# Reordering the SBUF tensors of a two-block transformer kernel (a 256-aligned layout against one whose large buffer starts 96 bytes off)

## The chip, the core and the metric

The kernel runs on one core of one Trainium2 chip, everything in float32 (indices in int32). The metric is the device time of one execution in microseconds, the median of several executions. Three executions of the kernel before took 2364.87, 2370.28 and 2371.98 us; the median is 2370.28 us.

## The reference, cut to what matters

Two blocks of two layers each run one after the other on 256 tokens of width 1024. The first block has a modulation (adaLN) from one conditioning vector, a mixer (pooling and windowed attention) and an expert layer in which each token fetches 128 experts by index; the second has four attention mixers and a dense MLP.

```python
for l in range(2):                                    # first block
    mod = silu(c) @ w_ada[l] + b_ada[l]               # 1024 x 6144
    h = rms_norm(x) * (1 + sc1) + sh1
    x = x + g1 * (mixer(h @ w_in[l]) @ w_out[l])
    h2 = rms_norm(x) * (1 + sc2) + sh2
    e, gate = peer_topk(h2 @ wq[l], subkeys[l])       # 128 experts for each token
    a = einsum('cd,ced->ce', h2, u[l][e])             # u, v: 16384 x 1024 each
    x = x + g2 * einsum('ce,ced->cd', gelu(a) * gate, v[l][e])
for l in range(2):                                    # second block
    x = x + mixers(rms_norm(x) @ w_in2[l]) @ w_out2[l]
    x = x + square(relu(rms_norm(x) @ w_up[l])) @ w_down[l]
return rms_norm(x)
```

## The kernel before, in words

The 256 tokens stand as two tiles of 128 partitions. Every SBUF tensor is declared once, at the start of `build` (L177 to L198), through `sb(name, n)`, which takes 128 partitions by `n` four-byte elements. The order of these declarations is the order in which the tensors lie in each partition. No tensor is reused through a pool that picks addresses; all views (`QK`, `RNG`, `HALF`, `S`, `kT`, `MT` and so on) are fixed slices of the declared tensors.

The largest tensor, `BIG`, holds 5120 elements of working space (`QK`) and then 12 slots of 2048 elements (`RNG`), 8 KB in each partition. A 13th slot is the first 2048 elements of `MOD`. Slots 0 to 7 and 13 take what GpSimd's queue fetches: first 48 blocks of `w_ada` (L447), then the expert rows (L454). One indirect DMA brings, for the 128 tokens of a tile, the row `uv[expert]`, which is the 1024 elements of `u` and the 1024 of `v`, 8 KB for each partition. There are 512 such fetches (4 passes of 128). Slots 8 to 11 take what SyncE loads (L325): the weights of the mixer and of the query projection, and in the second block all weights.

One expert step is: the row lands in a slot; VectorE forms the dot product of its first half with the token's `H` (L1620, output into `BIG`); ScalarE applies Gelu, the gate, and writes a diagonal matrix into `DG` (L1149, L966), reading the identity matrix that lies at the start of `CST`; TensorE multiplies the row's second half by that diagonal into PSUM (L513, two matmuls of 512 columns); then the slot is free and GpSimd issues the fetch that goes into it. The mixer and head steps of the next pass are interleaved with the expert steps by an order written out by hand (`WHEN`, `LATE`, `drive`). After the fourth pass the second block runs without gathers; its weights come through SyncE's queue into 12 slots in turn, two for each of the 16 MLP steps of a layer.

In the kernel before, `EPSC` takes 128 bytes at 16,512, and so `X` starts at 16,640, which is a multiple of 256. Every size up to and with `BIG` is a multiple of 256, so all of these start at one too. `PARB` does too, but its size isn't a multiple of 256, so `CST` (223,520) starts 32 bytes behind a multiple of 256 and `SC` (227,776) 192 behind one.

Of the kernel before, what the change touches and what calls it, by code (L numbers as in the profile page):

```python
# [20 lines left out]
PAR = 3720  # L21
# [3 lines left out]
C_ID, C_ND, C_ROPE, C_IOTA, C_SEL, C_END = 0, 128, 640, 1024, 1040, 1064  # L25
# [141 lines left out]
def build(nc, I, out):  # L167
    with ExitStack() as ctx:
        def sb(name, n, dt=F32):
            return ctx.enter_context(nc.sbuf_tensor(name, [128, n], dt))  # L170
# [1 line left out]
        T = Tally(lambda name: ctx.enter_context(nc.semaphore(name.replace(".", "_"))))  # L172
        up, at, last, landed = T.up, T.at, T.last, T.landed

        EPSC = sb("EPSC", 32)[:, 0:1]  # L177
        X = sb("X", 2048)[:, :].rearrange("p (t d) -> p t d", t=2)
        MOD = sb("MOD", 5120)[:, :]
        G2 = sb("G2", 1024)[:, :]  # L180
        ROWS = sb("ROWS", 256)[:, :]
        HT = sb("HT", 2048)[:, :].rearrange("p (c s) -> p c s", c=8)
        H = sb("H", 2048)[:, :].rearrange("p (t d) -> p t d", t=2)
        PRJ = sb("PRJ", 2560)[:, :]
        ONES = sb("ONES", 128)[:, :]
        ACC = sb("ACC", 1024)[:, :].rearrange("p (b n) -> p b n", b=2)
        DG = sb("DG", 4 * 128)[:, :].rearrange("p (b n) -> p b n", b=4)
        GATE = sb("GATE", 256)[:, :]
        AV = sb("AV", 256)[:, :]
        EID = sb("EID", 256, I32)[:, :]  # L190
        TV = sb("TV", 2 * 64)[:, :]
        TI = sb("TI", 2 * 64, U32)[:, :]
        TC = sb("TC", 256)[:, :]
        SKB = sb("SKB", 256)[:, :]
        BIG = sb("BIG", 5120 + SLOTS * SLOT)[:, :]
        PARB = sb("PARB", PAR)[:, :]
        CST = sb("CST", C_END)[:, :]
        SC = sb("SC", 384)[:, :]  # L198
        ZC = PARB[:, 384:888].rearrange("p (k m) -> p k m", k=8)
        CREP = PARB[:, 128:384].rearrange("p (k m) -> p k m", k=8)  # L200
        MC, BC, NC = PARB[:, 0:32], PARB[:, 32:64], PARB[:, 64:80]
        QK, RNG = BIG[:, 0:5120], BIG[:, 5120:5120 + SLOTS * SLOT]
        PS = ctx.enter_context(nc.psum_tensor("PS", [128, 8, 512], F32))

# [22 lines left out]
        S = QK[:, 4608:5120].rearrange("p (b i s) -> p b i s", b=2, i=2)  # L227
        prj1 = PRJ.rearrange("p (t n) -> p t n", t=2)
        g1, sh2, sc2 = (MOD[:, i * 1024:(i + 1) * 1024] for i in range(2, 5))
# [5 lines left out]
        AT = QK[:, 4096:5120].rearrange("p (b i s) -> p b i s", b=2, i=2)  # L235
        QF = PRJ[:, 0:768].rearrange("p (t i d) -> p t i d", t=2, i=4)
        KF = PRJ[:, 768:1536].rearrange("p (t i d) -> p t i d", t=2, i=4)
        VB = PRJ[:, 1536:2048].rearrange("p (t n) -> p t n", t=2)
        JD2 = PRJ[:, 2048:2304]
        RT, TMP = MOD[:, 0:1024], MOD[:, 1024:1344]  # L240
# [6 lines left out]
        def par1(k):  # L247
            return PARB[:, P1[k][0]:P1[k][0] + P1[k][1]]

# [68 lines left out]
        def sp_program(e):  # L318
# [33 lines left out]
            def head(l, t, h):  # L352
                if (l, t, h) == (1, 0, 0):
                    sp.wait_ge(*at("pe.sk", 0, 1, 7))
                    sp.e.dma_start(SKB, I["skT"][1]).then_inc(*landed("ld_sk", 1))
                if t == 0 or h > 1:
# [10 lines left out]
            sp.e.dma_start(G2[0:1, :], I["bada"][0:1, 5120:6144]).then_inc(*landed("ld_g2", 0))  # L367
            sp.e.dma_start(SKB, I["skT"][0]).then_inc(*landed("ld_sk", 0))
            sp.e.dma_start(ROWS[8:24, :], I["bada"][1:2, 2048:6144].rearrange("a (b n) -> (a b) n", n=256)).then_inc(*landed("ld_rows"))

# [138 lines left out]
        def pe_program(e):  # L509
# [34 lines left out]
            def spread(l, b, banks):  # L544
# [3 lines left out]
                if b < 8:  # L548
                    for c in range(2):
                        p = mm(PS[:, bk, 256 + c:257 + c], R[:, c * 128:(c + 1) * 128], ONES[:, 0:1], True, True)  # L550
                else:
                    p = mm(PS[:, bk, 256:512], ONES, R, True, True)
                p.then_inc(*up("pe.adb", l, b))
# [14 lines left out]
            def late():  # L568
# [3 lines left out]
                for c in range(2):  # L572
                    p = mm(PS[:, 2, 256 + c * 8:264 + c * 8], ROWS[:, c * 128:(c + 1) * 128], CST[:, C_SEL:C_SEL + 8], True, True)
                p.then_inc(*up("pe.adc"))
# [29 lines left out]
            def by_tokens(bk, t, w, width):  # L604
                wv = w[:, 0:8 * width].rearrange("p (k n) -> p k n", k=8)
                for k in range(8):
                    p = mm(PS[:, bk, 0:width], HT[:, k, t * 128:(t + 1) * 128], wv[:, k, :], k == 0, k == 7)
                return p
# [117 lines left out]
            def head(l, t, h):  # L726
                k = Clock()
                have_hT(l, t, 2)
                sk = SKB.rearrange("p (a n) -> p a n", a=2)
                wv = have(in_w, ("wq", l, t, h) if t == 0 or h > 1 else ("wq", l, 0, 7 - h)).rearrange("p (k n) -> p k n", k=8)  # L730
# [3 lines left out]
                for i in range(2):  # L734
                    yield from k.to(2 * i)
                    for c in range(8):
                        p = mm(PS[:, 7, i * 128:(i + 1) * 128], wv[:, c, i * 128:(i + 1) * 128],
                               HT[:, c, t * 128:(t + 1) * 128], c == 0, c == 7)
                p.then_inc(*up("pe.q", l, t, h))
# [7 lines left out]
            def experts(p, b):  # L747
# [9 lines left out]
                for hf in range(2):  # L757
                    m = mm(PS[:, hf, :], DG[:, (p * 128 + j) % 4, :], x[:, 1024 + hf * 512:1536 + hf * 512], j == 0, j == 127)
                m.then_inc(*up("pe.vsum", p, j))

            def project_A(l, t):
# [4 lines left out]
                for name, o, n in (("A0", 0, 192), ("A1", 192, 160)):  # L766
                    w = have(in_2, ("w2", l, name))[:, 0:8 * n].rearrange("p (k n) -> p k n", k=8)
                    for k in range(8):
                        p = mm(PS[:, bk, o:o + n], HT[:, k, t * 128:(t + 1) * 128], w[:, k, :], k == 0, k == 7)
                p.then_inc(*up("pe.A", l, t))  # L770
# [11 lines left out]
            def project(l, name, parts=(0, 1)):  # L782
# [11 lines left out]
                for z in parts:  # L794
                    zs = slice(z * 128, (z + 1) * 128)
                    for k in range(8):
                        if name in ("D0", "D1"):
                            p = mm(PS[:, bk, z * 256:(z + 1) * 256], w[:, k, zs], HT[:, k, :], k == 0, k == 7)
                        else:
                            p = mm(PS[:, bk, z * 256:(z + 1) * 256], HT[:, k, zs], w[:, k, :], k == 0, k == 7)  # L800
                if 1 in parts:
# [41 lines left out]
            def out2(l, s, t):  # L843
# [4 lines left out]
                for c in range(2):  # L848
                    for hf in range(2):
                        p = mm(PS[:, t * 2 + hf, :], HT[:, CHUNK[s] * 2 + c, t * 128:(t + 1) * 128], w[:, c, hf * 512:(hf + 1) * 512],  # L850
                               s == SECTIONS[0] and c == 0, s == SECTIONS[3] and c == 1)
# [110 lines left out]
        def act_program(e):  # L962
# [36 lines left out]
            def rms_in_hT(name, key, t, srcs, D):  # L999
# [5 lines left out]
                a.wait_ge(*last("a.c"))  # L1005
                a.e.activation(s, s, ACT.Sqrt, bias=EPSC, scale=1.0 / D).then_inc(*up("a.rms", *key))

            def rms(name, key, srcs, D, junk):
                s = sc(name, len(srcs))
                w = srcs[0].shape[-1]  # L1010
                for i, src in enumerate(srcs):
                    o = i * w % 1024
                    a.e.activation(junk[:, o:o + w], src, ACT.Square, accum_out=s[:, i:i + 1]).then_inc(*up("a.c"))
                    if o + w == 1024 or i == len(srcs) - 1:
                        a.wait_ge(*last("a.c"))
                a.e.activation(s, s, ACT.Sqrt, bias=EPSC, scale=1.0 / D).then_inc(*up("a.rms", *key))

# [38 lines left out]
            def pre(l, t):  # L1056
# [32 lines left out]
                a.wait_ge(*at("v.qks", l, t))  # L1089
                a.e.activation(s, s, ACT.Sqrt, bias=EPSC, scale=1.0 / 64).then_inc(*up("a.rms", "qk", l, t))  # L1090
                yield from k.to(WHEN["proj"] + 15)
# [31 lines left out]
            def head(l, t, h):  # L1123
# [9 lines left out]
                if n > 1:  # L1133
# [5 lines left out]
                a.wait_ge(*at("v.best", l, t, h))  # L1139
                a.e.activation(GATE[:, j:j + 16], V[:, 32:48], ACT.Exp, bias=V[:, 48:49], scale=1.0,  # L1140
                               accum_out=V[:, 49:50]).then_inc(*up("a.gate", l, t, h))

            def experts(p, b):
# [7 lines left out]
                a.wait_ge(*at("a.gelu", p, b - 1))  # L1151
                copy(AV[:, j:j + 1], AV[:, j:j + 1], GATE[:, j:j + 1]).then_inc(*up("a.gated", p, b - 1))
                if n > 3:
                    a.wait_ge(*at("pe.vsum", (n - 4) // 128, (n - 4) % 128))
                a.wait_ge(*at("a.gated", p, b - 1))
                copy(DG[:, n % 4, :], ident, AV[:, j:j + 1]).then_inc(*up("a.diag", p, b - 1))

# [11 lines left out]
            def latent(l, t):  # L1169
# [7 lines left out]
                a.wait_ge(*last("a.c"))  # L1177
                a.e.activation(s, s, ACT.Sqrt, bias=EPSC, scale=1.0).then_inc(*up("a.rms", "cn", l, t))

# [36 lines left out]
            for l in range(L):  # L1216
# [25 lines left out]
                for r in range(12):  # L1242
                    if r == 9:
                        squares(l, "a", ("m0", "m1"))
                        q = sc("yb", 8)
                        a.wait_ge(*at("v.subs", l))
                        a.e.activation(q, q, ACT.Sqrt, bias=EPSC, scale=1.0 / 64).then_inc(*up("a.rms", "yb", l))
                    if r == 10:
# [42 lines left out]
        def dve_program(e):  # L1291
# [63 lines left out]
            def late():  # L1355
# [3 lines left out]
                v.wait_ge(*at("ld_rows"))  # L1359
                tt(ROWS, PS[:, 2, 0:256], ROWS, ALU.add).then_inc(*up("v.rows"))  # L1360
                yield from k.to(WHEN["rows"] + 4)
# [4 lines left out]
                for i, (l, b) in enumerate(ADA[32:]):  # L1366
                    yield from k.to(LATE[i])
                    v.wait_ge(*at("pe.adb", *((l, b - 2) if b > 9 else (0, b + 14))))
                    ts(ACC[:, b % 2, 0:256], ROWS, CST[:, C_SEL + b:C_SEL + b + 1], None, ALU.mult, None).then_inc(*up("v.part", l, b))

# [178 lines left out]
            def head(l, t, h):  # L1549
# [18 lines left out]
                v.wait_ge(*at("v.top", l, t, h))  # L1568
                cd = TC[:, 0:256]
                tt(cd.rearrange("p (a b) -> p a b", a=16), bc(V[:, 0:16].unsqueeze(2), [128, 16, 16]),  # L1570
# [40 lines left out]
                own()  # L1611
                ts(GATE[:, j:j + 16], GATE[:, j:j + 16], V[:, 50:51], None, ALU.mult, None).then_inc(*up("v.gates", l, t, h))

# [19 lines left out]

            v.e.memset(ONES, 1.0)
            v.e.memset(MOD[:, 2048:5120], 0.0)
            v.e.memset(ROWS, 0.0)
            v.e.memset(G2, 0.0).then_inc(*up("v.zero"))
            v.e.memset(EPSC, EPS).then_inc(*up("v.eps"))
            v.wait_ge(*at("a.cond"))
# [351 lines left out]
```

## Time and profile before

| | |
|---|---|
| median of 3 executions | 2370.28 us (2364.87 to 2371.98) |
| the profiled execution | 2370.28 us, span 2368.5 us |
| around the span | 1.8 us |
| TensorE | 2117.9 us busy, 89% |
| VectorE | 1229.6 us, 52% |
| ScalarE | 822.9 us, 35% |
| GpSimd | 602.3 us, 25% |
| DMA | 767.01 MB, mean 324 GB/s |
| granted TensorE clock | 0.963 of full speed |

The span is the time between the first and the last instruction of the program. A busy share is one over the whole span, and the span has two parts of different kind: up to about 1601 us the experts are fetched, and from there the second block runs. So the shares of each part are read, not those of the whole.

### The profile page before, as it was taken

Reading aid. Unit: us, or ns where it says so; the run is one execution under the profiler, and the core shown is the slowest. Engines: PE = TensorE matmul, PEld = TensorE weight load, DVE = VectorE, ACT = ScalarE, POOL = GpSimd, SP = SyncE. Lnnn points to the kernel's source line nnn. Section 1 sums busy time; section 2 is a strip of 40 time slices with the busy share of each in tenths; the row PEclk is TensorE's granted clock in tenths of the full one; section 3 lists DMA queues with packets and bytes.
Section 4 is the critical chain, followed back from the end, with each engine's and each line's share of the span. In section 5 each row is a group of like instructions: output and inputs, shape, how many; then the busy total and the mean of one; then the engine's idle time right before and its main releaser. Section 6 shows DMA issues by size and latency. Waiting matters only on the chain.

```text
span 2368.5 us, 24191 instructions
## 1 busy us (share of the span) xinstructions
PE 2117.9 (89%) x8236; PEld 1251.3 (53%) x8236; DVE 1229.6 (52%) x2911; ACT 822.9 (35%) x2348; POOL 602.3 (25%) x564
## 2 busy tenths in 40 slices
PE   6779989888989888989987888889999999999998
PEld 4535545434545434645433333437856667766665
DVE  2327777776767676776876667754520002441001
ACT  1214554444554344554443444533310001331000
POOL 1123333444334343433444434420000000000000
PEclk9889999999999899999999999999899999999999
DMA  9999999999999999999999999983343432342420
GB/s 381 417 395 427 426 427 427 427 427 420 426 427 411 426 427 417 426 422 426 424 427 405 427 427 427 416 369 110 154 157 149 171 131 76 108 194 109 171 102 18
DMA packets 107711, 767.01 MB, mean 324 GB/s; under 512 B 12210, under 2 KB 12482, under 8 KB 15939
## 3 DMA queue, kind: packets, MB, share of 16 engines
q0 software_dynamic: 80640, 587.24, 59.1%
q1 hardware_dynamic: 26948, 178.23, 19.1%
q8 instruction: 65, 1.06, 0.2%
q14 instruction: 58, 0.48, 0.1%
HBM read 764.38 MB, written 1.05 MB: 323 GB/s over the span
## 4 chain that ended last, share of the span: by engine, by line
PE 58%; DMA 25%; DVE 9%; ACT 5%; issue 2%; POOL 0%; DVEq 0%; ACTq 0%; POOLq 0%
PE PS L513 56%; DMA BIG<-in_uv,EID 22%; DVE BIG L1620 3%; DMA BIG<-in_wada 3%; ACT DG L966 1%; DMA MOD<-in_uv,EID 1%; ACT L1149 1%; DVE BIG L1313 1%; DVE SC L1389 1%; PE PS L625 1%; PE PS L592 1%; ACT AV L966 1%; ACT BIG L1035 0%; DVE X L1303 0%; DVE BIG L1299 0%
## 5 line engine op out<-in xcount | busy, mean ns | idle before, releaser
L513 PE MATMUL PS<-BIG,DG 128*128 128x512 f32 x1820 | 888.8, 625 | 159.7 <-ACT DG L966 141.2
L1620 DVE CUSTOM_DVE_ANT_0 BIG<-BIG,H 128x1024 f32<-128x1024 f32 x455 | 558.1, 1227 | 357.7 <-DMA BIG<-in_uv,EID 327.8
L454 POOL DMA_INDIRECT BIG<-in_uv,EID x455 | 510.1, 1121 | 766.7 <-PE PS L513 744.1
L513 PEld LDWEIGHTS PS<-BIG,DG 128*128 128x128 f32 x1820 | 332.3, 195 | 611.2 <-issue 297.2
L513 PEld LDWEIGHTS PS<-HT,BIG 128*128 128x128 f32 x2304 | 350.3, 193 | 76.4 <-issue 47.8
L513 PE MATMUL PS<-HT,BIG 128*128 128x128 f32 (+1 forms) x2304 | 383.6, 323 | 7.3 <-DVE HT L1299 3.5
L1149 ACT ACTIVATE AV<-AV 128x1 f32<-128x1 f32 x512 | 103.2, 201 | 666.9 <-DVE AV L1620 662.9
L513 PE MATMUL PS<-BIG,HT 128*128 128x256 f32 (+3 forms) x1216 | 299.7, 404 | 10.6 <-DVE HT L1299 3.6
L513 PE MATMUL PS<-BIG 128*128 128x512 f32 (+7 forms) x792 | 282.4, 528 | 1.8 <-DVE BIG L1299 1.8
L513 PEld LDWEIGHTS PS<-BIG,HT 128*128 128x128 f32 x1216 | 230.9, 196 | 80.0 <-issue 48.8
L1303 DVE TENSOR_TENSOR BIG<-BIG 128x256 f32<-128x256 f32 (+1 forms) x96 | 49.4, 515 | 383.5 <-ACT BIG L1284 381.3
L966 ACT ACTIVATE DG<-CST,AV 128x128 f32<-128x128 f32 x512 | 205.5, 401 | 48.9 <-ACT AV L966 1.5
L513 PEld LDWEIGHTS PS<-BIG 128*128 128x128 f32 (+3 forms) x792 | 134.6, 194 | 128.8 <-issue 124.0
L966 ACT ACTIVATE AV<-AV,GATE 128x1 f32<-128x1 f32 x512 | 150.7, 294 | 18.6
L1284 ACT ACTIVATE BIG<-PS 128x512 f32<-128x512 f32 x32 | 19.1, 597 | 383.9 <-PE PS L513 383.9
L513 PE MATMUL PS<-MOD,DG 128*128 128x512 f32 x228 | 113.8, 623 | 9.4 <-ACT DG L966 9.1
L1620 DVE CUSTOM_DVE_ANT_0 BIG<-MOD,H 128x1024 f32<-128x1024 f32 x57 | 70.1, 1229 | 41.0 <-DMA MOD<-in_uv,EID 36.8
L454 POOL DMA_INDIRECT MOD<-in_uv,EID x57 | 66.6, 1168 | 72.8 <-PE PS L513 69.0
L966 ACT ACTIVATE BIG<-PS 128x256 f32<-128x256 f32 (+6 forms) x122 | 52.9, 446 | 85.9 <-PE PS L625 45.9
L513 PEld LDWEIGHTS PS<-MOD,DG 128*128 128x128 f32 x228 | 42.8, 199 | 67.0 <-issue 39.5
L1149 ACT ACT_TABLE_LOAD x52 | 66.7, 1283 | 0.9
L513 PE MATMUL PS<-BIG,PARB 128*32 128x256 f32 x688 | 54.5, 453 | 13.4 <-DMA BIG<-in_wada 9.8
(173 smaller groups left out, 1271.4 us busy)
## 6 DMA issues: line engine op xcount, KB each, us to landing
BIG<-in_wada POOLq DMA_DIRECT2D x43, 1024.0 KB
BIG<-in_win SPq DMA_DIRECT2D x36, 1024.0 KB, 6.0
BIG<-in_wup SPq DMA_DIRECT2D x32, 1024.0 KB, 6.9
BIG<-in_wdn SPq DMA_DIRECT2D x32, 1024.0 KB, 4.8
BIG<-in_wq SPq DMA_DIRECT2D x28, 1024.0 KB
BIG<-in_wout SPq DMA_DIRECT2D x24, 1024.0 KB, 5.4
BIG<-in_uv,EID POOLq DMA_INDIRECT x455
MOD<-in_wada POOLq DMA_DIRECT2D x5, 1024.0 KB
```

Source lines behind the costliest of these rows:

```text
L454: pool.e.indirect_dma_start(out=slot(u), out_offset=None, in_=I[f"uv{l}"], in_offset=bass.IndirectOffsetOnAxis(ap=EID[:, t * 128 + j:t * 1 ...
L513: return pe.e.matmul(dst, a, b, start=start, stop=stop)
L592: p = pe.e.transpose(PS[:, bk, c * 128:(c + 1) * 128], H[:, t, (c4 * 4 + c) * 128:(c4 * 4 + c + 1) * 128], ident)
L625: p = pe.e.transpose(PS[:, bk, x * 128:(x + 1) * 128], P[:, i, kc * 128:(kc + 1) * 128], ident)
L966: return a.e.activation(dst, src, ACT.Copy, scale=scale)
L1149: a.e.activation(AV[:, j:j + 1], AV[:, j:j + 1], ACT.Gelu).then_inc(*up("a.gelu", p, b - 1))
L1284: a.e.activation(AT[:, b % 2], PS[:, singles.where[("up", l, b)], :].rearrange("p (i s) -> p i s", i=2), ACT.Relu).then_inc(*up("a.relu", ...
L1303: return v.e.tensor_tensor(dst, a, b, op)
L1313: return v.e.scalar_tensor_tensor(out=dst, in0=a, scalar=s, in1=b, op0=op0, op1=op1)
L1389: v.e.reduce_max(mx, src, AX).then_inc(*up("v.c"))
L1620: v.e.tensor_tensor_reduce(out=JD, in0=slot(u)[:, 0:1024], in1=H[:, t, :], scale=1.0, scalar=0.0, op0=ALU.mult, op1=ALU.add, accum_out=AV[ ...
```

## The change

The change reorders the declarations of the SBUF tensors and makes `EPSC` one element instead of the first of 32. Nothing else: every instruction, every wait and every DMA is the same, in the same order, with the same sizes, and only the SBUF addresses differ.

```diff
-        EPSC = sb("EPSC", 32)[:, 0:1]
         X = sb("X", 2048)[:, :].rearrange("p (t d) -> p t d", t=2)
         MOD = sb("MOD", 5120)[:, :]
         G2 = sb("G2", 1024)[:, :]
         ROWS = sb("ROWS", 256)[:, :]
+        PARB = sb("PARB", PAR)[:, :]
         HT = sb("HT", 2048)[:, :].rearrange("p (c s) -> p c s", c=8)
         H = sb("H", 2048)[:, :].rearrange("p (t d) -> p t d", t=2)
         PRJ = sb("PRJ", 2560)[:, :]
+        CST = sb("CST", C_END)[:, :]
         ONES = sb("ONES", 128)[:, :]
         ACC = sb("ACC", 1024)[:, :].rearrange("p (b n) -> p b n", b=2)
         DG = sb("DG", 4 * 128)[:, :].rearrange("p (b n) -> p b n", b=4)
+        SC = sb("SC", 384)[:, :]
         GATE = sb("GATE", 256)[:, :]
         AV = sb("AV", 256)[:, :]
         EID = sb("EID", 256, I32)[:, :]
         TV = sb("TV", 2 * 64)[:, :]
         TI = sb("TI", 2 * 64, U32)[:, :]
         TC = sb("TC", 256)[:, :]
+        EPSC = sb("EPSC", 1)[:, :]
         SKB = sb("SKB", 256)[:, :]
         BIG = sb("BIG", 5120 + SLOTS * SLOT)[:, :]
-        PARB = sb("PARB", PAR)[:, :]
-        CST = sb("CST", C_END)[:, :]
-        SC = sb("SC", 384)[:, :]
```

(The views `CREP`, `ZC`, `MC`, `BC`, `NC` of `PARB` move with it.) Where the tensors start, in bytes of a partition, and how far behind a multiple of 256 and of 64 that is:

| tensor | before | behind 256 / 64 | after | behind 256 / 64 |
|---|---|---|---|---|
| `X` | 16,640 | 0 / 0 | 16,512 | 128 / 0 |
| `MOD` (13th slot) | 24,832 | 0 / 0 | 24,704 | 128 / 0 |
| `H` | 58,624 | 0 / 0 | 73,376 | 160 / 32 |
| `HT` | 50,432 | 0 / 0 | 65,184 | 160 / 32 |
| `PRJ` | 66,816 | 0 / 0 | 81,568 | 160 / 32 |
| `DG` | 81,664 | 0 / 0 | 100,672 | 64 / 0 |
| `BIG` (slots 1 to 12, `QK`) | 89,856 | 0 / 0 | 110,432 | 96 / 32 |
| `PARB` | 208,640 | 0 / 0 | 50,304 | 128 / 0 |
| `CST` | 223,520 | 32 / 32 | 91,808 | 160 / 32 |
| `SC` | 227,776 | 192 / 0 | 102,720 | 64 / 0 |

A slot is 8192 bytes and `QK` 20,480, both multiples of 256, so each of the 12 slots starts as far behind a multiple of 256 as `BIG` does.

## Rows read from the trace of the kernel before

**Rows 1.** Windows: two stretches; columns in the first row, DMA share of 16 engines.

```profile
core 0: us, PE busy (x) PEld busy (x) DVE busy (x) ACT busy (x) POOL busy (x), PEclk, DMA share, GB/s
60.00:1601.00 1541.00, 1342.95 (x4827) 702.29 (x4828) 1046.87 (x2535) 689.75 (x1980) 592.00 (x541) 0.96 1.00 420
1601.00:2368.00 767.00, 734.04 (x3102) 519.90 (x3101) 168.24 (x340) 122.68 (x346) 0.00 (x0) 0.98 0.33 126
```

**Rows 2.** DMA view, 60 to 1601 us: GB/s in 40 slices; queues: packets, MB, share.

```profile
GB/s 426 366 425 426 426 427 426 427 427 427 426 427 419 423 427 427 426 410 419 426 427 427 413 425 427 419 427 426 423 427 426 395 427 426 426 427 427 416 421 337
...
q0 software_dynamic: 78741, 573.36, 88.6%
q1 hardware_dynamic: 10971, 72.92, 11.4%
```

**Rows 3.** Waits, longest first: engine line waited for, us, times, longest.

```profile
POOL BIG L454 <- PE PS L513: 744.1, 402, 7.6
ACT AV L1149 <- DVE AV L1620: 662.9, 396, 38.5
...
DVE BIG L1620 <- DMA BIG<-in_uv,EID: 327.8, 282, 35.5
```

**Rows 4.** DMA view, 597 to 602 us: the load of `poolw` into an aligned slot.

```profile
q1 hardware_dynamic: 144, 0.26, 13.6%
```

**Rows 5.** DMA view, 1331 to 1335 us: the load of `sm` into `CST`.

```profile
DMA packets 346, 1.68 MB, mean 421 GB/s; under 512 B 45, under 2 KB 45, under 8 KB 173
...
q1 hardware_dynamic: 149, 0.28, 17.9%
```

**Rows 6.** DMA view, 6.1 to 9.7 us: the load of `cst` into `CST`.

```profile
q1 hardware_dynamic: 129, 0.54, 36.8%
```

**Rows 7.** Source L1303, VectorE: duration ns min/median/max, first and last start, shapes.

```profile
L1303 DVE TENSOR_TENSOR BIG<-BIG,CST x64: 424/424/427, 138.0 to 1523.5; 128x256 f32<-128x256 f32 x64
L1303 DVE TENSOR_TENSOR TC<-TV x32: 424/425/427, 134.4 to 1512.7; 128x256 f32<-128x256 f32 x32
```

**Rows 8.** Source L1308, VectorE, the same columns.

```profile
L1308 DVE TENSOR_SCALAR H<-X,SC x4: 753/754/812, 13.3 to 914.4; 128x1024 f32<-128x1024 f32 x4
```

**Rows 9.** Source L1620, VectorE, the dot product.

```profile
L1620 DVE CUSTOM_DVE_ANT_0 BIG<-BIG,H x455: 1224/1226/1300, 180.2 to 1591.1; 128x1024 f32<-128x1024 f32 x152
L1620 DVE CUSTOM_DVE_ANT_0 BIG<-MOD,H x57: 1224/1226/1298, 193.7 to 1586.2; 128x1024 f32<-128x1024 f32 x57
```

**Rows 10.** Tile CST and tile BIG: TensorE and ScalarE.

```profile
L966 ACT ACTIVATE DG<-CST,AV x512: 401/401/404, 182.1 to 1593.0; 128x128 f32<-128x128 f32 x171
...
L592 PE MATMUL PS<-CST,H x160: 272/273/477, 14.2 to 2146.0; 128*128 128x128 f32 x160
...
L513 PE MATMUL PS<-SKB,BIG x128: 272/275/422, 128.0 to 1493.9; 128*128 128x128 f32 x128
```

**Rows 11.** Tile BIG: the matmul on a fetched row.

```profile
L513 PE MATMUL PS<-BIG,DG x1820: 592/592/1222, 182.6 to 1594.8; 128*128 128x512 f32 x182
```

**Rows 12.** Windows: the two MLPs of the second block, columns as in Rows 1.

```profile
1763.00:1976.00 213.00, 212.41 (x768) 140.54 (x769) 14.26 (x21) 11.00 (x19) 0.00 (x0) 1.00 0.35 132
2147.00:2361.00 214.00, 213.89 (x768) 140.83 (x768) 13.81 (x20) 11.00 (x19) 0.00 (x0) 1.00 0.27 103
```

More of the change, by code:

```diff
@@ L187, in build @@
         DG = sb("DG", 4 * 128)[:, :].rearrange("p (b n) -> p b n", b=4)
+        CREP = PARB[:, 128:384].rearrange("p (k m) -> p k m", k=8)
+        ZC = PARB[:, 384:888].rearrange("p (k m) -> p k m", k=8)
+        MC, BC, NC = PARB[:, 0:32], PARB[:, 32:64], PARB[:, 64:80]
+        SC = sb("SC", 384)[:, :]
         GATE = sb("GATE", 256)[:, :]
@@ L193, in build @@
         TC = sb("TC", 256)[:, :]
+        EPSC = sb("EPSC", 1)[:, :]
         SKB = sb("SKB", 256)[:, :]
         BIG = sb("BIG", 5120 + SLOTS * SLOT)[:, :]
-        PARB = sb("PARB", PAR)[:, :]
-        CST = sb("CST", C_END)[:, :]
-        SC = sb("SC", 384)[:, :]
-        ZC = PARB[:, 384:888].rearrange("p (k m) -> p k m", k=8)
-        CREP = PARB[:, 128:384].rearrange("p (k m) -> p k m", k=8)
-        MC, BC, NC = PARB[:, 0:32], PARB[:, 32:64], PARB[:, 64:80]
         QK, RNG = BIG[:, 0:5120], BIG[:, 5120:5120 + SLOTS * SLOT]
```

## The prediction

> **What bounds the kernel now.** I read the windows first, because the program has two parts of different kind. From 60 to 1601 us the 16 DMA engines are busy for a share of 1.00 while they move 420 GB/s; from 1601 us to the end the share is 0.33 and TensorE is busy for 734.04 of 767 us [rows 1]. The DMA view of the first part shows 426 to 428 GB/s in most slices, with a few dips to 366, 395 and 407 to 423, so the engines have no idle time to give [rows 2]. 88.6% of it is GpSimd's queue, the expert rows. The list of waits seems to say something else: its longest entry is GpSimd's fetch waiting for TensorE (744.1 us), then ScalarE waiting for VectorE's dot product (662.9), and only then VectorE waiting for the fetched row (327.8) [rows 3]. The reader should see a ring here: the fetch waits for its slot, the slot was filled late, and what each turn of the ring costs is the DMA engines' time for 1 MB. Since they are full, the waits are the slack of the others. So in the first part an edit counts only if it changes the time that the DMA engines need for a packet; in the second part only if it changes TensorE's, which is busy for 212.41 of 213 and 213.89 of 214 us in the two MLPs [rows 12].
>
> **The change part by part.** No instruction, wait or DMA is added, removed or moved. What changes is where operands and destinations start. All 12 slots of `BIG` go from a multiple of 256 bytes to 96 behind one (32 behind a multiple of 64); the 13th slot goes to 128 behind a multiple of 256. `H`, `HT`, `PRJ` go to 32 behind a multiple of 64. `EPSC`, one element a partition in both, only moves. Three prices are to be found, and the kernel before holds a control for each, because its `CST` already starts 32 bytes behind a multiple of 64, the same place within 64 bytes as `BIG` after.
>
> *1. The DMA packet.* One packet carries one partition's piece. First the price of an aligned one. In 597 to 602 us SyncE's queue holds 144 packets, 0.26 MB: 128 of 2048 bytes (`poolw`) and 16 tiny ones that signal completion; 13.6% of 16 x 5 us is 10.88 us [rows 4]. The gather queue in the first part holds 573.36 MB, which is 69,990 packets of 8192 bytes, and 8751 tiny ones; 88.6% of 16 x 1541 us is 21,845 us [rows 2]. With a time of s for a tiny packet, and s + k x bytes for any, these two rows give s = 8.3 ns, k = 0.0370 ns a byte, 84.0 ns for 2048 bytes and 311.1 ns for 8192. Now the two loads whose destination is 32 bytes off. The `sm` load: 149 packets, 0.28 MB, 17.9% of 16 x 4 us = 11.46 us; 0.28 MB is 128 of 2048 bytes and two of 8192 from the load behind it, and 19 tiny ones. (11,456 - 2 x 311 - 19 x 8.3) / 128 = 83.4 ns [rows 5]. Aligned it would be 84.0; the last digit of the shares is worth 0.3 ns. The `cst` load: 129 packets, 36.8% of 16 x 3.6 us = 21.2 us, 165.6 ns for each of 128 packets of 4256 bytes [rows 6]. The line above gives 8.3 + 4256 x 0.0370 = 165.8. Both ran in the middle of full DMA traffic, and in the `sm` window the core still moved 421 GB/s. So a destination 32 bytes off costs nothing that I can see. Not shown is a destination 96 or 128 off, and not a stream of thousands of such packets, in which a backlog could build up that 8 packets an engine don't show.
>
> Here a rule of the Trainium skill speaks against this change. "DMA: Bandwidth & Descriptors", section "How a descriptor splits into AXI transactions", says that a descriptor which doesn't start at a multiple of 256 bytes begins with a transaction from the boundary below it, and that the bytes ahead of the start cost time though they aren't used. For 8192 bytes from 96 off that makes 259 beats of 32 bytes in place of 256. This trace disagrees on the source side, and slightly on the destination's: the rows of `cst` in HBM are 4256 bytes apart, so they start at all multiples of 32 behind a multiple of 256, 112 on the mean, which by the rule and k would be 169.9 ns where 165.6 was measured; `sm` by the rule would be 85.2 ns where 83.4 was measured. By the rule the sum would be 2388, by the rows 2370.
>
> The bounds, from rows alone. Below: a packet gets shorter by at most nothing from its own start (83.4 against 84.0 is inside two roundings), so 0. Above: 96 more bytes to move, 3.55 ns, or in the worst case one more full 256 bytes, 9.5 ns. Up to 1601 us each engine moves (573.36 + 72.92) MB / 8192 / 16 = 4931 packets in the window and 4% more ahead of it, say 5120. That is 0 to 18.2 us, 48.6 us in the worst case. I take 0, the value of the two nearest rows. After 1601 us the DMA share of 0.33 would hide any of these.
>
> *2. VectorE and ScalarE operands.* The comparison of the same operation and size with and without an operand in `CST`: 424 ns median with `CST`, 425 without [rows 7]. ScalarE's diagonal already reads `CST` in every one of its 512 steps, at 401 ns with a maximum of 404 [rows 10]. The dot product will read `BIG` and `H` 32 bytes off in place of 0; it takes 1226 ns and stands beside a DMA turn of 8 x 311.1 + 8.3 = 2497 ns [rows 9], so even a few ns more would be covered by the DMA engines. What no row shows off by 32 is the operation that takes 754 ns for 1024 elements, faster than the others' pace (425 for 256) [rows 8]. If it fell to the pace of the dot product, that is 4 x 0.47 = 1.9 us, on the path ahead of each mixer step, of which only the first is not under a gather. I take 0; the bounds are 0 and 1.9 us.
>
> *3. TensorE operands.* Transposes read `CST` and take 273 ns median; a matmul of the same 128x128 that reads aligned tensors takes 275 [rows 10]. So no cost: 0. The upper end I set at 16 more columns (the 64 bytes within which the operand is now off) in each matmul of 512 columns (592 ns [rows 11]): 18.5 ns. In the first part the DMA engines hide that; in the MLPs, 768 + 768 matmuls, half of them of 256 columns, it would be about 28 us [rows 12]. The control excludes it for 128 columns, to about 2 ns.
>
> The sum: 2368.5 us span + 1.8 around it + 0 + 0 + 0 = 2370.3 us. The profiled execution is the median one itself, 2370.28, so I predict 2370.
>
> **The rivals.**
>
> *A. The fetches pay for their start (slower).* Each 8 KB packet into a slot pays for the 96 bytes between the boundary and its start. The place is the gather part, where nothing covers it. For it: the part is bound by exactly this resource, and the only property that the move takes from every slot is a start at a multiple of 256. Against it: rows 5 and 6. It decides from about 1.4 ns a packet, since 5120 x 1.4 = 7 us, which is 0.3% of 2370 and about what a measurement of this kernel can tell from no change. Time: 2370 + 18 = 2388. With 32 bytes in place of 96 it would be 2376, in the worst case 2419.
>
> *B. Placement relieves the dips (faster).* The first part moves 647.32 MB; at 427 GB/s in place of 420 it would take 1516 us and not 1541. If some of the dips came from two streams meeting at equal low address bits, since in the kernel before all of `X` to `BIG` start at a multiple of 256, a spread layout could give up to 25 us, 2345. Against it: the dot product under full DMA traffic is 1224 at least, 1226 median [rows 9], so reads and writes of SBUF don't visibly disturb each other; and the dips are few and stand apart, as drops for lack of a free slot would. A third of it would be 2362.
>
> *C. TensorE's or VectorE's reads pay (slower).* 2370 + 28 + 2 = 2400. Against it: rows 7 and 10, which show the same offset within 64 bytes at no cost.
>
> *D. The change isn't what it says.* Padding could undo the 96 bytes. It doesn't: each tensor starts at the next multiple of 32, by the table of starts, and `BIG` stays at 96.
>
> **How the numbers follow.** No change: 0.48. A: 0.39, since the controls are short loads with another offset and its place is the one that matters most. B: 0.09. C: 0.04. D is contained in no change. The forecast's own range is 2363 to 2377. A ends on the same side for all its prices but the smallest, so slower by over 0.3% gets 0.39 - 0.03 + 0.04 + 0.02 (a loss of an unnamed kind) = 0.42; faster 0.09; the rest, 0.49, is within 0.3%. The range of 8 in 10 must reach A's price of 96 bytes, 2388, with some margin for the spread of the runs; below it needs only the forecast's own range and the small end of B. So 2361 to 2393, which leaves out the worst case of A, most of C and the far end of B.
>
> **What would show it right or wrong.** Right: in the DMA view of 60 to 1601 us the gather queue again takes about 311 ns for an 8 KB packet, the slices again read 426 to 428 GB/s, and the last fetched row lands at the same time as before. A is right if this comes to 314 or 315 ns and the slices read about 422, with the second part unchanged in length. C is right if the 512-column matmul's minimum is above 592 or the dot product's median above 1226, and the MLP windows are longer than 213 and 214 us. The VectorE operation of rows 8 shows the second price alone. The prediction is wrong in its main step if the gather part changes in length by over 7 us; it is wrong in its reading of what bounds the kernel if the packet gets dearer and the end doesn't move.

## The result and the profile after

The kernel after takes 2385.54 us (median of 4 executions, 2383.68 to 2389.89), the kernel before 2367.95 us in the 4 executions of it by then: a ratio of 1.0076, with an interval of 1.0053 to 1.0099. It is slower by 0.76%, 18 us, where I had forecast no change (2370, and 2361 to 2393 as the range). The forecast of no change was wrong; the time came out near the 2388 of rival A.

The profiled execution took 2386.07 us, with a span of 2384.3 us, 15.8 more than before. First the windows, cut at the end of the gathers as in [rows 1], which now is at 1616 us and not at 1601:

```profile
60.00:1616.00 1556.00, 1340.36 (x4814) 697.99 (x4815) 1045.88 (x2534) 687.90 (x1977) 589.93 (x540) 0.96 1.00 415
1616.00:2384.00 768.00, 734.82 (x3114) 520.83 (x3112) 168.27 (x340) 125.20 (x349) 0.00 (x0) 0.98 0.34 127
```

The first part grew by 15 us and the second stayed (768 against 767 us, TensorE busy for 734.82 against 734.04). The DMA engines are as full as before (share 1.00) but move 415 GB/s in place of 420. The DMA view of the same stretch shows it slice by slice, against [rows 2]:

```profile
GB/s 420 386 421 421 420 421 421 422 421 421 421 420 410 420 421 421 421 398 417 421 421 421 416 420 421 421 421 418 402 421 422 386 422 421 421 421 421 421 410 330
...
q0 software_dynamic: 78677, 572.86, 88.9%
```

The reader should look at the value that most slices have, not at the mean: 427 became 421, everywhere. For 1 MB an engine handles 8 packets, so 1,048,576 bytes / 427 GB/s = 2456 ns and / 421 GB/s = 2491 ns differ by 35 ns, 4.4 ns a packet. The queue's row says the same: (0.889 x 16 x 1556 us - 8748 x 8.3 ns) / 69,929 packets = 315.5 ns, against 311.1. The last gathered row's dot product began at 1608.5 us, in place of 1591.1:

```profile
L1618 DVE CUSTOM_DVE_ANT_0 BIG<-BIG,H x455: 1224/1226/1286, 178.3 to 1608.5; 128x1024 f32<-128x1024 f32 x152
```

The engines' prices are untouched: the dot product above has the 1224 and 1226 ns of [rows 9], and by the rows below the fast VectorE operation of [rows 8], the diagonal and the transposes of [rows 10] and the 512-column matmul of [rows 11] have the times they had:

```profile
L1306 DVE TENSOR_SCALAR H<-X,SC x4: 753/753/806, 13.3 to 923.2; 128x1024 f32<-128x1024 f32 x4
```

```profile
L511 PE MATMUL PS<-BIG,DG x1820: 592/592/1222, 180.7 to 1612.3; 128*128 128x512 f32 x182
...
L964 ACT ACTIVATE DG<-CST,AV x512: 401/401/404, 180.2 to 1610.4; 128x128 f32<-128x128 f32 x171
...
L590 PE MATMUL PS<-CST,H x160: 272/273/449, 14.2 to 2161.7; 128*128 128x128 f32 x160
```

### The profile page after: what moved, and what is told of

It reads as the page before. It is cut to its first block, busy times and chain, and to the rows that moved or that the text cites. A ratio compares the mean times of both kernels' runs of the same rounds, so it can differ in the third digit from the quotient of the medians.

```text
span 2384.3 us, 24191 instructions
## 1 busy us (share of the span) xinstructions
PE 2117.2 (89%) x8236; PEld 1248.3 (52%) x8236; DVE 1229.3 (52%) x2911; ACT 823.8 (35%) x2348; POOL 600.8 (25%) x564
## 4 chain that ended last, share of the span: by engine, by line
PE 56%; DMA 28%; DVE 8%; ACT 5%; issue 2%; POOL 1%; DVEq 0%; ACTq 0%; SPq 0%; POOLq 0%
PE PS L511 54%; DMA BIG<-in_uv,EID 23%; DMA MOD<-in_uv,EID 3%; DVE BIG L1618 3%; ACT DG L964 1%; DMA BIG<-in_wada 1%; PE PS L590 1%; ACT L1147 1%; DVE BIG L1311 1%; PE PS L623 1%; DVE SC L1387 1%; ACT AV L964 1%; POOL BIG L452 1%; DVE X L1301 0%; DVE H L1311 0%
## 5 line engine op out<-in xcount | busy, mean ns | idle before, releaser
L1618 DVE CUSTOM_DVE_ANT_0 BIG<-BIG,H 128x1024 f32<-128x1024 f32 x455 | 557.9, 1226 | 378.4 <-DMA BIG<-in_uv,EID 355.0
L452 POOL DMA_INDIRECT BIG<-in_uv,EID x455 | 504.1, 1108 | 785.4 <-PE PS L511 758.4
```

The lines of the kernel that those rows point to most:

```text
L452: pool.e.indirect_dma_start(out=slot(u), out_offset=None, in_=I[f"uv{l}"], in_offset=bass.IndirectOffsetOnAxis(ap=EID[:, t * 128 + j:t * 1 ...
L1618: v.e.tensor_tensor_reduce(out=JD, in0=slot(u)[:, 0:1024], in1=H[:, t, :], scale=1.0, scalar=0.0, op0=ALU.mult, op1=ALU.add, accum_out=AV[ ...
```

## The experiments

Each was timed in several rounds beside the kernel before on the same chip.

**Where the slots start.** Seven kernels move `MOD` and `BIG`, and with them all 13 slots, against the layout after. Five of them do it with p free bytes ahead of the two:

```diff
         X = sb("X", 2048)[:, :].rearrange("p (t d) -> p t d", t=2)
-        MOD = sb("MOD", 5120)[:, :]
         G2 = sb("G2", 1024)[:, :]
...
         SKB = sb("SKB", 256)[:, :]
+        sb("PAD", p // 4)
+        MOD = sb("MOD", 5120)[:, :]
         BIG = sb("BIG", 5120 + SLOTS * SLOT)[:, :]
```

with p = 32, 64, 96, 128 and 160 for starts 128, 160, 192, 224 and 0 behind a multiple of 256. For the start 0, `SC` also moves behind `BIG` and has 376 elements, since the space ends there; for 64, `EPSC` moves behind `BIG` and there is no pad; for 32, `EPSC` and `PARB` do. In this last one the tensors that stood behind `PARB` move up too: `H`, `HT`, `PRJ` and `CST` start 128 behind a multiple of 256, in place of 160.

Start 0. 

> The layout after, with MOD moved to stand directly ahead of BIG and 160 bytes left free ahead of both, so that all 13 slots start at a multiple of 256 bytes; X, H, HT, PRJ, CST, DG and the others stay as far behind such a multiple as in the kernel after. Theory 1 (each 8 KB packet pays for the bytes between the multiple of 256 below its start and the start): the whole loss goes, ratio to the kernel before 0.998 to 1.002, 421 GB/s in the full slices of the gather part go back to 427. Theory 2 (each packet pays a fixed price when it doesn't start at a multiple of 256) and theory 3 (it pays when it starts off a multiple of 64) say the same here. Theory 4 (the loss comes from the operands of the engines, H, HT, PRJ, CST, not from the slots): still 1.0076, 421 GB/s.

Start 32. 

> All 13 slots start 32 bytes behind a multiple of 256. With k = 0.0370 ns a byte and 5120 packets an engine up to the end of the gathers, as in the prediction: theory 1 gives 1.2 ns a packet, 6 us, ratio 1.0026. Theory 2 (fixed price) gives the loss of the kernel after, 17.6 us, 1.0076, and so does theory 3 (off a multiple of 64). My bet is theory 1.

Start 128. 

> All 13 slots start 128 bytes behind a multiple of 256, which is a multiple of 64 and of 128. Theory 1: 4.7 ns a packet, 24 us, ratio 1.0102. Theory 2: 1.0076. Theory 3: no loss, 1.000.

Start 224. 

> All 13 slots start 224 bytes behind a multiple of 256 (32 behind one of 64). Theory 1: 8.3 ns a packet, 42 us, ratio 1.018, full slices at about 416 GB/s. Theory 2 and theory 3: 1.0076.

The first four showed that the price has one height and not a slope, and the theory was put anew (theory 5) before the next three.

Start 64. 

> All 13 slots start 64 bytes behind a multiple of 256. So far: 0 behind gives 1.0008, 32 gives 1.0098, 96 (the kernel after) and 128 give 1.0076, 224 gives 1.0105; full slices 427, 419, 421, 421, 420 GB/s. Theory 2 as it now stands (5): a packet off a multiple of 256 is written as one more piece than it needs, for a fixed 3.8 ns, and about 1.1 ns more where one of its two end pieces has only 32 bytes (start 32 or 224 behind). It expects 421 GB/s in the full slices and 1.0076. Theory 6 (two prices by whether the start is off a multiple of 64 or not, 96 being an outlier) expects 421 too. Theory 1 (bytes ahead of the start) expects 1.005.

Start 160. 

> All 13 slots start 160 bytes behind a multiple of 256 (32 behind one of 64), the mirror of 96: end pieces of 96 and 160 bytes. Theory 5: 421 GB/s, 1.0076. Theory 6: 419 to 420 GB/s, 1.010. Theory 1: 1.0128.

Start 192. 

> All 13 slots start 192 bytes behind a multiple of 256, the mirror of 64: end pieces of 64 and 192 bytes. Theories 5 and 6: 421 GB/s and 1.0076, the same as 64 behind. Theory 1: 1.0153.

| start behind a multiple of 256 | ratio to before | interval | most slices, GB/s |
|---|---|---|---|
| 0 (`off0`) | 1.0008 | 0.9996 to 1.0021 | 427 |
| 32 | 1.0098 | 1.0082 to 1.0115 | 419 |
| 64 | 1.0074 | 1.0050 to 1.0098 | 421 |
| 96 (the kernel after) | 1.0076 | 1.0053 to 1.0099 | 421 |
| 128 | 1.0076 | 1.0058 to 1.0095 | 421 |
| 160 | 1.0082 | 1.0063 to 1.0102 | 421 |
| 192 | 1.0094 | 1.0073 to 1.0114 | 421 |
| 224 | 1.0105 | 1.0085 to 1.0124 | 419 |

The slices of three of them, from the DMA view of 60 to 1600 us: start 0, then 128, then 224.

```profile
GB/s 426 402 425 427 426 427 426 426 428 426 427 426 415 426 426 427 426 406 425 427 427 426 411 426 426 421 426 427 424 426 428 390 426 427 426 427 427 427 414 341
```

```profile
GB/s 420 411 422 421 420 422 421 421 421 421 421 421 418 422 421 419 418 407 402 421 421 420 393 421 420 420 422 421 422 421 421 390 420 421 421 420 421 411 412 400
```

```profile
GB/s 418 389 420 419 418 420 419 420 419 421 419 420 416 415 418 419 420 419 402 419 419 419 375 419 418 419 420 419 420 419 419 412 383 419 420 418 421 418 419 419
```

Theory 1, the bytes between the boundary and the start, is out, and with it my bet at 32: it wanted 1.0026 at 32, 1.0102 at 128 and 1.018 at 224. Theory 3, the multiple of 64, is out: 64, 128 and 192 cost as much as 96. Theory 4, the engines' operands, is out: with `H`, `HT`, `PRJ` and `CST` left off and only the slots put back, the loss is gone. What stands is theory 2: every start off a multiple of 256 costs nearly the same, about 4.4 ns a packet, and about one more when one of the two end pieces, the one up to the first multiple of 256 or the one behind the last, has only 32 bytes. For the second height the slices are coarse: 419 GB/s are 2503 ns a MB, 5.9 ns a packet, but one GB/s is already worth 0.7 ns. The gather queue's rows are finer. Start 64, then start 32, both from 60 to 1600 us:

```profile
q0 software_dynamic: 78605, 572.36, 89.7%
```

```profile
q0 software_dynamic: 78330, 570.40, 89.7%
```

Worked out as for the kernel after, they give 315.3 and 316.4 ns, 4.2 and 5.3 above the aligned 311.1. By the times alone the two heights (1.0074 to 1.0094 against 1.0098 and 1.0105) would not be safe, since the intervals overlap; the slices and these rows carry it.

**The slots alone, in the layout before.**

The order of the declarations is now this, with the pads in elements (`SC` has 376 of them):

```
PAD 32, X, G2, ROWS, HT, H, PRJ, ONES, ACC, DG, GATE, AV, EID, TV, TI, TC, SKB, PARB, EPSC, PAD 8, MOD, BIG, CST, SC
```

> The other half of the change alone, turned round: X, H, HT, PRJ, DG, ACC and the small tensors start at a multiple of 256 bytes as in the kernel before, and only the 13 slots (MOD and BIG, and CST) start 96 behind one. If the slots carry the whole loss: 1.0076 and 421 GB/s. If a part came from the engines' operands: below 1.006.

Measured: 1.0079 (1.0059 to 1.0099), 421 GB/s in most slices. With `off0` this closes the account from both sides: without the slots' start the loss goes, and with it alone it comes back. `CST` stands at 96 here as well, and so does `QK`; in `off16` and `off4` below both keep to multiples of 32 bytes, and only the slots leave them.

**Source or destination.** The table of expert rows is shifted by 96 bytes in HBM, under slots at 0 and under slots at 96:

```diff
-        o[f"uv{l}"] = np.concatenate([a["peer_u"][l], a["peer_v"][l]], axis=1)
+        uv = np.concatenate([a["peer_u"][l], a["peer_v"][l]], axis=1)
+        o[f"uv{l}"] = np.concatenate([np.zeros(24, f), uv.reshape(-1), np.zeros(2024, f)]).reshape(16385, 2048)
...
                         in_offset=bass.IndirectOffsetOnAxis(ap=EID[:, t * 128 + j:t * 128 + j + 1], axis=0),
+                        element_offset=24,
```

> The kernel before with the expert table shifted by 96 bytes in HBM (24 elements ahead of the first row, and a gather that starts 24 elements in), so that every gathered row is read from 96 bytes behind a multiple of 256 and written to a multiple of 256. Theory W (the price is one of writing to SBUF): no loss, 1.000 to 1.002, 427 GB/s in full slices. Theory R (either side off a multiple of 256 costs, as the 3 more beats of the page's rule would): 1.0076, 421 GB/s. Theory D (what costs is source and destination off by different amounts): 1.0076 too.

> The kernel after with the same shifted table: source and destination both 96 bytes behind a multiple of 256. Theory W: as the kernel after, 1.0076, 421 GB/s. Theory R: 1.0076 or twice that. Theory D: the loss goes, 1.000, 427 GB/s.

Measured: 1.0004 (0.9990 to 1.0019) for source 96 and slots 0, and 1.0089 (1.0072 to 1.0107) for 96 and 96. The slices, from 60 to 1600 us, of the first and of the second:

```profile
GB/s 427 405 425 426 426 426 428 425 427 427 427 426 417 426 426 427 426 406 426 426 428 426 412 427 426 426 427 422 421 426 427 391 427 426 427 426 427 418 415 339
```

```profile
GB/s 420 410 421 421 420 421 421 421 422 421 421 421 403 421 420 420 421 415 408 420 422 420 408 420 422 416 421 421 412 421 421 392 419 421 421 421 422 407 397 409
```

427 and 421. So it is the writing of SBUF alone (theory W). Reading HBM from 96 off is free, and it doesn't help that source and destination are off by the same.

**Per packet or per byte.** Each gather is cut in two of 4096 bytes a partition, from two tables:

```diff
-                    pool.e.indirect_dma_start(
-                        out=slot(u), out_offset=None, in_=I[f"uv{l}"],
-                        in_offset=bass.IndirectOffsetOnAxis(ap=EID[:, t * 128 + j:t * 128 + j + 1], axis=0),
-                    ).then_inc(*landed(f"ga{u}", p, j))
+                    for z in range(2):
+                        pool.e.indirect_dma_start(
+                            out=slot(u)[:, z * 1024:(z + 1) * 1024], out_offset=None, in_=I[f"{'uv'[z]}{l}"],
+                            in_offset=bass.IndirectOffsetOnAxis(ap=EID[:, t * 128 + j:t * 128 + j + 1], axis=0),
+                        ).then_inc(*landed(f"ga{u}", p, j))
```

> The kernel before with each gather cut in two of 4096 bytes a partition (u row and v row from tables of their own), slots at a multiple of 256. The base for the next run. A packet of 4096 bytes takes 8.3 + 151.6 ns, so a row takes 16 x 159.9 + 2 x 8.3 ns an engine, 2575 in place of 2497: about 1.02, if GpSimd keeps up with twice 1.1 us of issue a row; if it doesn't, GpSimd is the bound and the time is above 1.05.

> The kernel after with each gather cut in two of 4096 bytes. Against split_dst0: a fixed price of 3.8 ns a packet counts twice a row, about 9200 packets an engine, 35 us, so 1.015 above split_dst0 (mean packet 4 ns dearer). A price by bytes (1.2% of the packet) gives 1.0076 above it, mean packet 2 ns dearer. If GpSimd is the bound, the two runs agree, and only the packets' times tell the theories apart.

Measured: 1.0168 (1.0149 to 1.0187) and 1.0261 (1.0243 to 1.0279), medians of 2401.83 and 2425.43 us, 24 us apart. The slices of the first and of the second:

```profile
GB/s 426 399 423 420 419 421 419 420 421 420 398 394 416 407 420 420 421 420 395 386 420 419 421 420 419 420 421 420 382 380 393 420 420 421 420 419 419 419 375 406
```

```profile
GB/s 420 385 420 411 410 410 412 410 411 412 409 411 409 395 410 411 411 411 378 364 410 410 409 411 410 411 411 412 409 378 378 406 410 410 410 409 410 410 409 400
```

420 became 410: 1 MB takes 2497 and 2558 ns, 61 ns apart on 16 packets, 3.8 ns each. For 8 packets of 8192 bytes it was 35 ns. A price by bytes would have left the 35 ns as they were, so in the main it is a price by packet. It isn't quite the same for every size: 4096 bytes pay a little less than 8192, and a load of 2048 bytes in such a stream paid 1.8 ns (below). The time moved by less than my 35 us: by 24. Both kernels have deep dips that the uncut ones don't have (380 to 398 GB/s in `split_dst0`), and GpSimd is busy for 1131 us in place of 602 (whole profile of `split_dst0` and of the kernel before), so not all of their gather part is bound by the packets; how much, I haven't taken apart.

**Starts that aren't a multiple of 32.** In the kernel before, `BIG` gets 8 more elements, and the slots move on inside it:

```diff
-        BIG = sb("BIG", 5120 + SLOTS * SLOT)[:, :]
+        BIG = sb("BIG", 5120 + 8 + SLOTS * SLOT)[:, :]
...
-        QK, RNG = BIG[:, 0:5120], BIG[:, 5120:5120 + SLOTS * SLOT]
+        QK, RNG = BIG[:, 0:5120], BIG[:, 5124:5124 + SLOTS * SLOT]     # off16; 5121 for off4
```

> The kernel before with BIG 8 elements longer and its 12 slots moved on by 4 elements inside it, so that they start 16 bytes behind a multiple of 256 (the slot in MOD stays at 0, one in nine of the gathers). Theory P (one more piece, dearer when an end piece is short): as 32 behind, 419 GB/s in full slices where all slots are in BIG, ratio 1.009. Theory Q (also a price for each piece that isn't on 32 bytes): a packet of 8192 bytes has 256 such pieces of 32 bytes; if each costs even a tenth more, 31 ns a packet, 1.065.

> The same with the slots moved on by 1 element, 4 bytes behind a multiple of 256. Theory P: 1.009 to 1.011, as 16 behind. Theory Q: 1.065 or more.

The slot in `MOD`, one in nine of the gathers, stays at a multiple of 256; `PARB`, `CST` and `SC` move by 32 bytes.

Measured: 1.0115 (1.0086 to 1.0143) and 1.0106 (1.0078 to 1.0134), both with 419 GB/s in most slices. Theory P holds and Q falls: 4 or 16 bytes off costs what 32 off costs, so the price belongs to the packet's ends and not to its inner pieces.

## Why the prediction was wrong, step by step

*What bounds the kernel*: right. The gather part is bound by the DMA engines' time for a packet and passes it on. 4.4 ns on 5120 packets is 22.5 us; the median moved by 17.6, the profiled span by 15.8. About 1 us of the rest is in the start-up (below); the other 4 or so aren't taken apart. The second part, whose DMA share is 0.33, showed nothing, as said.

*Step 1, the DMA packet*: this is the step that failed. I took 0, "the value of the two nearest rows", for a destination off a multiple of 256, and it is 4.4 ns in the gather stream. Rival A, which I gave 0.39, had the place and the end right (2388), but by the wrong rule: it priced 96 bytes at 3.55 ns, and the price doesn't grow with the 96. That its number came so near is luck: at 32 off it said 2376 and at 224 it would have said 2412, where the ratios measured give 2391 and 2393.

Why did the two controls show nothing? The `sm` load of [rows 5] and the `cst` load of [rows 6] wrote to 32 off, the dearer kind, and their packets took the aligned time. I misread the first of them a little: the packets of the kept trace are 128 of 2048 bytes, one of 13,328 and 20 tiny ones, not two of 8192 and 19 tiny ones, and so it is 84.2 ns and not 83.4, against 84.0 aligned. That doesn't change what it says: 0.2 ns, where the stream pays over 5. I had noted the gap, "a backlog could build up that 8 packets an engine don't show", and then gave it no weight. The kernel after allows the reverse test. There, in 601 to 606 us, the `poolw` load of [rows 4] goes to a slot that is 96 off, in the middle of a stream that is off as a whole:

```profile
q1 hardware_dynamic: 144, 0.26, 13.9%
```

13.9% of 80 us is 11.12 us, and (11,120 - 16 x 8.3) / 128 = 85.8 ns, in place of 84.0. The `sm` load separates a packet's own start from that of its neighbours, because `CST` is 160 off both in `off0`, where the stream is aligned, and in the kernel after, where it is off. In `off0` (1327.7 to 1331.7 us; again with one packet of 13,328 bytes and 23 tiny ones), then in the kernel after (1344.8 to 1349.0 us; 20 tiny ones):

```profile
q1 hardware_dynamic: 152, 0.28, 17.9%
```

```profile
q1 hardware_dynamic: 148, 0.26, 16.5%
```

That is 84.1 and 85.3 ns. So the same load to the same offset pays nothing in an aligned stream and about 1 ns in one that is off. Whether an aligned packet would pay there too, no run shows.

In the second part, where the engines have gaps, no price stands out. Before (1700 to 2360 us), with the slots at 32 (1721 to 2381 us), and in the kernel after (1716 to 2376 us):

```profile
q1 hardware_dynamic: 11863, 83.20, 33.0%
```

```profile
q1 hardware_dynamic: 11952, 83.50, 33.2%
```

```profile
q1 hardware_dynamic: 11884, 83.29, 33.3%
```

3485 us for 10,156 times 8192 bytes is 343 ns, 3506 us for 10,193 is 344 ns, and 3516 us for 10,167 is 346 ns. A mean of this stretch is too coarse to settle a few ns: for the packets of 8192 bytes after 1720 us it is 342 ns in each of the four traces with aligned slots, and between 338 and 344 in the twelve with slots off. The middle packet is the better gauge: 309 ns in all sixteen, while in the gather part (kernels with uncut rows) it is 309 ns with aligned slots and 312 to 314 with slots off. So a packet's own time doesn't carry the price of its own write; it shows when the stream around it is full and off. That something between reading and writing takes up the lag of a packet or a short load is what this suggests; no run measured how much it holds, so the mechanism stays argued, while the two facts (no price that can be seen in an aligned or a loose stream, the full price in a full stream that is off) are shown.

The comparison on the source side was sound. The rows of `cst`, which start at all multiples of 32 in HBM, said that a source may be off for free, and `src96_dst0` confirms it. The mistake was on the destination's side: to let two loads in an aligned stream speak for a stream that is off as a whole. The Trainium skill, "DMA: Bandwidth & Descriptors", section "How a descriptor splits into AXI transactions", makes an off packet one transaction longer (by its rule 33 in place of 32) and also 3 beats longer here, and it words this for what a transaction reads. The runs differ from it on the reading side, where 96 off cost nothing (1.0004, 427 GB/s). On the writing side one more piece would fit them, though no run counts pieces; the beats don't fit: between 64 and 192 off most slices read 421 GB/s, though by the beats 192 would cost three times as much as 64.

*Steps 2 and 3, the engines' operands*: right, all at 0, by the rows above and by `off0`, in which `H`, `HT` and `PRJ` are still 32 off and nothing is lost. Rival C is out, rival D too.

*Rival B, relief of the dips*: not in the gather part, where the full slices all fell. The stage before it is another matter, below.

*The range and the chances*: the range held the time, by its upper end, which was there for rival A. The forecast itself was wrong because a price whose ends were 0 and 48 us, in the resource that bounds the kernel, was settled by two controls of 8 packets an engine.

## What to carry to other kernels

When a DMA stream bounds a kernel, start each SBUF destination at a multiple of 256 bytes, and put tensors whose size isn't a multiple of it (a one-element constant, a parameter row) behind the buffers, or pad them. In the gather stream of this kernel it is worth about 4 to 5 ns a packet, 1.4 to 1.7% of an 8 KB packet, 2.4% of a 4 KB one, and nothing that could be seen where the DMA engines have gaps. To price something in a full stream, use a stretch of the trace that is itself a full stream of it: the time of a single packet in a short load isn't the rate that a long one gets.

## What I had not expected of the hardware

The loads at the start ran slower in three of the four kernels with slots at a multiple of 256. In 14 to 34 us the kernel before moves 389 GB/s with full DMA engines, `off0` 378 and `split_dst0` 390, while the kernel after moves 420:

```profile
14.00:34.00 20.00, 16.14 (x168) 9.80 (x168) 1.84 (x11) 3.38 (x9) 0.00 (x0) 0.97 1.01 389
```

```profile
14.00:34.00 20.00, 16.21 (x169) 9.82 (x170) 2.89 (x14) 4.58 (x12) 0.00 (x0) 0.97 1.02 420
```

The other kernels with slots off have 411 (`only96`) to 420 there. But `src96_dst0`, whose slots are at 0 and whose loads in this stretch are the same as in the kernel before, has 419. So the start of the slots alone doesn't decide it, and each is one profile. It is worth 8% of 20 us or so, 1 to 2 us, and at 60 us about 1 of them is left between the kernels before and after; this is part of why the time moved by less than the packets' sum. What causes it stays open.
